# Four layers' experts as three fp32r passes a product, with split weights and four landing buffers

## The reference

```python
combine = jnp.sum(jax.nn.one_hot(idx, N_EXPERTS, dtype=jnp.float32) * gsel[..., None], axis=-2)
...
gate, up = jnp.split(jnp.einsum('ld,edf->lef', xs, w_gu), 2, axis=-1)     # 1024 -> 2 x 256
hid = jax.nn.silu(gate) * up * cw[..., None]
return jnp.einsum('lef,efd->ld', hid, w_down)                             # 256 -> 1024
```

## Time and profile before

| | us |
|---|---|
| median of 3 runs (2869.59 to 2881.02) | 2874.03 |
| the profiled execution | 2871.9 |
| its span, first to last instruction | 2870.1 |
| PE busy | 2560.3 (89%) |
| weight loads of PE busy | 1879.5 (65%) |
| DVE busy | 1432.8 (50%) |
| POOL busy | 796.8 (28%) |
| ACT busy | 753.7 (26%) |

### The profile page before, as it was taken

One profiled execution on the slowest core, in us unless ns is written; L12 is line 12 of the kernel. 1 busy time (PEld: TensorE's weight loads), 2 busy tenths in 40 slices (PEclk: granted clock), 3 DMA queues, 4 the chain that ended last, 5 costly groups with the idle time before them and its releaser, 6 DMA issues.

```text
span 2870.1 us, 30129 instructions
## 1 busy us (share of the span) xinstructions
PE 2560.3 (89%) x11915; PEld 1879.5 (65%) x11915; DVE 1432.8 (50%) x1956; ACT 753.7 (26%) x1265; POOL 796.8 (28%) x429
## 2 busy tenths in 40 slices
PE   5779889998898979999988977789999799889997
PEld 3779864445887778744458966675444699864444
DVE  6446553334746776533446489874333426740013
ACT  1133130012553451300023344422100333130111
POOL 3356400001543434000015478730000357500000
PEclk8889989998999999899989988989999899989998
DMA  7533639892331236398925311144999143438880
GB/s 267 173 118 92 212 147 348 331 369 98 107 118 35 83 93 184 148 351 330 368 81 182 118 36 36 34 176 176 345 344 349 35 129 103 147 117 297 301 297 35
DMA packets 291851, 524.41 MB, mean 183 GB/s; under 512 B 9472, under 2 KB 141056, under 8 KB 291328
## 3 DMA queue, kind: packets, MB, share of 16 engines
q1 hardware_dynamic: 288256, 519.33, 51.5%
q10 hardware_dynamic: 3456, 3.15, 0.3%
HBM read 517.73 MB, written 4.72 MB: 182 GB/s over the span
## 4 chain that ended last, share of the span: by engine, by line
PE 73%; DVE 14%; ACT 4%; DMA 3%; issue 3%; POOL 2%; SPq 0%; ACTq 0%; DVEq 0%
PE ps L1895 23%; PE ps L1912 12%; PE ps L1642 6%; PE ps L1643 6%; PE ps L1644 6%; DVE macc L1984 3%; PE ps L1707 2%; POOL wlo L1574 2%; DVE uw L1335 2%; PE ps L1665 1%; PE ps L1833 1%; PE ps L1667 1%; PE ps L1666 1%; PE ps L1857 1%; PE ps L1858 1%
## 5 line engine op out<-in xcount | busy, mean ns | idle before, releaser
L1574 POOL TENSOR_TENSOR wlo<-ring,whi 128x1024 fp32r<-128x1024 f32 x202 | 533.2, 2655 | 1467.5 <-ACT whi L1441 1467.5
L1895 PE MATMUL ps<-ring,xg 128*128 128x512 f32 x1536 | 702.7, 595 | 0.0
L1895 PEld LDWEIGHTS ps<-ring,xg 128*128 128x128 f32 x1536 | 280.5, 190 | 296.7 <-issue 296.3
L1984 DVE SCALAR_TENSOR_TENSOR macc<-ring,cond_s,macc 128x1024 f32<-128x1024 f32 x322 | 440.9, 1429 | 10.6 <-DMA ring<-w_mod 10.6
L2202 DVE SCALAR_TENSOR_TENSOR hid<-ps,cws,sg 128x256 f32<-128x256 f32 x96 | 46.4, 483 | 652.7 <-ACT sg L1535 652.7
L1912 PE MATMUL ps<-ring,hidt 128*128 128x512 f32 x768 | 353.4, 604 | 2.3 <-ACT hidt L1510 2.3
L1642 PE MATMUL ps<-hh,whi 128*128 128x384 f32 x840 | 301.3, 359 | 29.6 <-POOL wlo L1574 16.9
L1643 PE MATMUL ps<-hl,whi 128*128 128x384 f32 x840 | 289.9, 345 | 0.0
L1644 PE MATMUL ps<-hh,wlo 128*128 128x384 f32 x840 | 289.5, 345 | 0.0
L1441 ACT ACTIVATE whi<-ring 128x1024 fp32r<-128x1024 f32 x202 | 207.0, 1054 | 312.0 <-DMA ring<-gmlp_w_out 111.7
L1912 PEld LDWEIGHTS ps<-ring,hidt 128*128 128x128 f32 x768 | 147.7, 194 | 185.2 <-issue 185.2
(11 more groups left out here) (358 smaller groups left out, 4040.9 us busy)
## 6 DMA issues: line engine op xcount, KB each, us to landing
ring<-moe_w_gu SPq DMA_DIRECT2D x192, 1024.0 KB, 8.2
ring<-w_mod SPq DMA_DIRECT2D x96, 1024.0 KB, 8.2
ring<-moe_w_down SPq DMA_DIRECT2D x96, 1024.0 KB, 6.2
ring<-gmlp_w_in SPq DMA_DIRECT2D x32, 1024.0 KB, 5.8
ring<-ssd_w_in SPq DMA_DIRECT2D x21, 1024.0 KB, 5.2
ring<-hgrn_w_in SPq DMA_DIRECT2D x20, 1024.0 KB, 5.3
ring<-gmlp_w_out SPq DMA_DIRECT2D x16, 1024.0 KB, 5.8
ring<-ssd_w_out SPq DMA_DIRECT2D x8, 1024.0 KB, 6.2
```

The source lines that it names most:

```text
L1574: pool.tensor_tensor(split_sub(wlo, s0), raw_sub(s0), split_sub(whi, s0).bitcast(F32), ALU.subtract).then_inc(S["lo_ready"], 1)
L1895: ins = pe.matmul(ps[:, s % 2, :], xg[:, w, k, :], whole(what, s, 4)[:, k % 4, :], start=(k == 0), stop=(k == KD - 1))
L1984: ins = dve.scalar_tensor_tensor(out=macc[:, v, :], in0=w[:, k, :], scalar=by, in1=macc[:, v, :], op0=ALU.mult, op1=ALU.add)
```

## The change

`SPLIT` names the layers whose experts are done in the new way: all four. Their weight chunks become narrow, as in the mixers, with two subs each (a sub of A or B is two rows of 128x512, a sub of D one row of 1024), and so do the modulation chunks that ride along: four landing slots for all of them. ACT makes the highs; of the lows, POOL makes those of first subs and DVE those of second subs (`low` in the DVE block; vector_lows and pool_lows count them apart, which is why every wait for lo_ready in the mixers now goes by pool_lows). A slot of an expert chunk is free once both of its lows are made, that of a modulation chunk once its four multiply-adds are. xg and hidt get a high part (ACT, as before) and a low part by DVE (xgl, hidtl). PE does three passes for each product. DVE's four multiply-adds are parted: two before hid of their step, two after. The core of the diff (the renamed waits and the parts for layers outside SPLIT are left out):

```diff
+SPLIT = (0, 1, 2, 3)
...
+    rows_of = -1 if l not in SPLIT else 2 if what == "D" else 4
+    part(("mod", l + 1) if what == "M" else (l, what), 1, 0 if what == "M" else rows_of, l not in SPLIT)
...
+    vector_lows, pool_lows = [0], [0]
+    for s in order_of:
+        by_vector = chunk_rows[s // 2] in (2, 4) and s % 2 == 1
+        vector_lows.append(vector_lows[-1] + by_vector)
+        pool_lows.append(pool_lows[-1] + (not by_vector))
...
+    elif chunk_rows[p] in (2, 4):
+        sp.wait_ge(S["lo_ready"], pool_lows[nth[2 * p] + 2])
+        sp.wait_ge(S["low_ready"], vector_lows[nth[2 * p] + 2])
...
+    def expert_used(eng, l, what, s):
+        if l in SPLIT:
+            eng.wait_ge(S["sub_done"], nth[sb((l, what), 2 * s + 1)] + 1)
+        else:
+            eng.wait_ge(S["moe_used"], used[places[l, what][s]])
...
+    ahead = lambda what, i: feed(sb((l, what), i) + 3) if l in SPLIT and i >= 0 else None
     for s in range(STEPS):
+        ahead("A", 2 * s)
+        ahead("A", 2 * s + 1)
         if s:
             hidden_over(s - 1)
-        act.wait_ge(S["moe_used"], used[places[l, "B"][s]])
+        ahead("B", 2 * s)
+        ahead("B", 2 * s + 1)
+        expert_used(act, l, "B", s)
         if s >= 2:
             act.wait_ge(S["hid_ready"], n0 + s - 1)
         act.activation(sg[:, s % 2, :], ps[:, s % 2, 0:DE], ACT.Silu).then_inc(S["sg_ready"], 1)
+        ahead("D", 2 * s - 2)
+        ahead("D", 2 * s - 1)
...
+    if vector_lows[n + 1] > vector_lows[n]:
+        return
...
+    claim(at_bank, "xgl_ready", 16 * SPLIT.index(l) + 2 * k + part + 1)
...
+    def wide_product(out, xhi, xlo, s0, half, first, last):
+        cut = slice(512 * half, 512 * half + 512)
+        hi, lo = whi[:, nth[s0] % SPL, cut], wlo[:, nth[s0] % SPL, cut]
+        pe.matmul(out, xhi, hi, start=first, stop=False)
+        pe.matmul(out, xhi, lo, start=False, stop=False)
+        return pe.matmul(out, xlo, hi, start=False, stop=last)
...
+    s0 = sb((l, what), 2 * s + k // 2 % 2)
+    if k % 2 == 0:
+        low_in(s0)
+    ins = wide_product(ps[:, s % 2, :], xgh[:, w, k, :], xgl[:, w, k, :], s0, k % 2, k == 0, k == KD - 1)
+    if k % 2:
+        ins.then_inc(S["sub_done"], 1)
+    if s and k == 1:
+        hidden_over(s - 1)
...
+    for k in range(2):
+        s0 = sb((l, "D"), 2 * s + k)
+        low_in(s0)
+        for h in range(2):
+            ins = wide_product(ps[:, OUT_BANKS[w % 2][h], :], hidth[:, s % 2, k, :], hidtl[:, s % 2, k, :], s0, h,
+                               e == 0 and k == 0, e == EG - 1 and k == 1)
+        ins.then_inc(S["sub_done"], 1)
+    return
...
+    def low(l, what, i):
+        n = nth[sb((l, what), i)]
+        s0 = order_of[n]
+        dve.wait_ge(S["hi_ready"], n + 1)
+        dve.tensor_tensor(split_sub(wlo, s0), raw_sub(s0), split_sub(whi, s0).bitcast(F32), ALU.subtract).then_inc(S["low_ready"], 1)
...
+    def rows_low(k):
+        if l in SPLIT:
+            dve.wait_ge(S["xg_ready"], 16 * l + 2 * k + 2)
+            for part, (a, b) in enumerate(((0, NG), (NG, NW))):
+                dve.tensor_tensor(xgl[:, a:b, k, :], ps[:, 2 * ((k + 1) % 2) + part, 0:(b - a) * P].rearrange("p (w n) -> p w n", n=P),
+                                  xgh[:, a:b, k, :].bitcast(F32), ALU.subtract).then_inc(S["xgl_ready"], 1)
...
+    def hidden_rest(s):
+        dve.wait_ge(S["hidt_ready"], n0 + s + 1)
+        dve.tensor_tensor(hidtl[:, s % 2, :, :].rearrange("p a n -> p (a n)"), ps[:, 2, (s % 2) * DE:(s % 2 + 1) * DE],
+                          hidth[:, s % 2, :, :].rearrange("p a n -> p (a n)").bitcast(F32), ALU.subtract).then_inc(S["hidtl_ready"], 1)
...
+    if l in SPLIT and s:
+        low(l, "B", 2 * s + 1)
+        hidden_rest(s - 1)
+        if e == 1 and w:
+            window_low(w - 1)
+        low(l, "D", 2 * s - 1)
+    if l in SPLIT and s in mods:
+        mod_chunk(MODC * (l + 1) + MOD_GROUP + mods[s], range(0, 2))
...
+    if l in SPLIT and s + 1 < STEPS:
+        low(l, "A", 2 * s + 3)
     if last_of(s - 2):
         mod_take(6 * (l + 1) + 1 + mods[s - 2] // MOD_GROUP)
     if s in mods:
-        mod_chunk(MODC * (l + 1) + MOD_GROUP + mods[s])
+        mod_chunk(MODC * (l + 1) + MOD_GROUP + mods[s], range(2, 4) if l in SPLIT else range(4))
```

More of the change, by code:

```diff
@@ L266, in trunk @@
         olo = ar("olo", [P, NW, D], F32R, 24)
+        xgh = ar("xgh", [P, NW, KD, P], F32R, 48)
+        xgl = at("xgl", [P, NW, KD, P], F32R, hoff)
         spread = ar("spread", [P, NT, NW * P], F32R, 24)
@@ L279, in trunk @@
         hidt = yr("hidt", [P, 2, 2, P], F32, 4)
+        hidth = yr("hidth", [P, 2, 2, P], F32R, 4)
+        hidtl = yr("hidtl", [P, 2, 2, P], F32R, 9)
         srow = yr("srow", [P, T], F32, 6)
@@ L1409, in split_waits @@
             for l in range(DEPTH - 1):
-                if n == nth[end_of_experts(l)]:
+                if l not in SPLIT and n == nth[end_of_experts(l)]:
                     eng.wait_ge(S["moe_used"], used[places[l, "D"][-1]])
@@ L1904, in down @@
                     w, e = divmod(s, EG)
[L1905 to L1906 removed]
+                    if l not in SPLIT:
+                        chunk_in(pe, places[l, "D"][s])
+                    pe.wait_ge(S[turned], t0 + s + 1)
                     if e == 0:
@@ L1965, in _, with mod_chunk @@
             link = chain.link
-            def mod_chunk(m):
+            def mod_chunk(m, parts=range(4)):
                 q, steps = m % MOD_GROUP, 4 * (MOD_GROUP * group_of_mac(m // MOD_GROUP) + m % MOD_GROUP)
                 c = mod_at[steps // 4]
-                chunk_in(dve, c)
                 w = ring[:, slot_of[c], :].rearrange("p (k n) -> p k n", k=2)
-                if m == 0:
-                    dve.wait_ge(S["cond_ready"], 1)
-                elif q == 0:
-                    dve.wait_ge(S["mod_summed"], m // MOD_GROUP)
-                for k in range(2):
-                    for v in range(2):
-                        by = cond[:, 2 * q + k, v:v + 1]
-                        if q == 0 and k == 0:
-                            ins = dve.tensor_scalar(macc[:, v, :], w[:, k, :], by, None, ALU.mult)
-                        else:
-                            dve.wait_ge(S["mac_step"], steps + 2 * k + v - 1)
-                            ins = dve.scalar_tensor_tensor(out=macc[:, v, :], in0=w[:, k, :], scalar=by, in1=macc[:, v, :],
-                                                           op0=ALU.mult, op1=ALU.add)
-                        ins.then_inc(S["mac_step"], 1)
@@ new lines, in mod_chunk @@
+                if 0 in parts:
+                    chunk_in(dve, c)
+                    if m == 0:
+                        dve.wait_ge(S["cond_ready"], 1)
+                    elif q == 0:
+                        dve.wait_ge(S["mod_summed"], m // MOD_GROUP)
+                for k, v in (divmod(i, 2) for i in parts):
+                    by = cond[:, 2 * q + k, v:v + 1]
+                    if q == 0 and k == 0:
+                        ins = dve.tensor_scalar(macc[:, v, :], w[:, k, :], by, None, ALU.mult)
+                    else:
+                        dve.wait_ge(S["mac_step"], steps + 2 * k + v - 1)
+                        ins = dve.scalar_tensor_tensor(out=macc[:, v, :], in0=w[:, k, :], scalar=by, in1=macc[:, v, :],
+                                                       op0=ALU.mult, op1=ALU.add)
+                    ins.then_inc(S["mac_step"], 1)
@@ L2107, in route @@
                 pairs = rt[:, 2:4, :, :].rearrange("p a t e -> p (a t e)")[:, 0:72].rearrange("p (g e) -> p g e", e=6)
+                if l in SPLIT:
+                    low(l, "A", 1)
+                    low(l, "B", 1)
                 dve.wait_ge(S["route_ready"], l + 1)
```

90 lines of the change are left out of this document (56 added, 34 removed).

## The result

| | before | after |
|---|---|---|
| median | 2872.01 us (2869.59 to 2881.02, 4 runs) | 3381.45 us (3373.25 to 3387.71, 4 runs) |
| span of the profiled execution | 2870.1 us | 3377.1 us |
| PE busy, DVE busy | 2560.3, 1432.8 us | 2571.8, 2226.2 us |
| ACT busy, POOL busy | 753.7, 796.8 us | 1324.6, 1583.4 us |

The ratio of the times is 1.1755 (95% interval 1.1732 to 1.1777): 17.6% slower, as forecast.

A forecast was written before the change was run, and what follows sets the result against it. TensorE (PE) was taken to bound the kernel now; after the change, loads and POOL/DVE turns would. 2871.9 us + 488 (layers 0 to 2) + 19 (layer 3) + 4 (sorted rows) = 3383, stated as 3380 us, range 3110 to 3500.

The forecast's parts named there:

- The load path: Layers 0 to 2: moe_w_down loads wait for multiply-adds queued behind the previous moe_w_down's low on DVE; three-step period 51.9 us, chance 0.55.
- D0: The moe_w_down chunk of step 0 in the hand-built three-step period; its load, sent second, lands at 9.0 us.
- D1: The next step's moe_w_down chunk in that period; its load waits for the second pair of multiply-adds, lands at 27.7 us.
- the first rival: Expert stages, layers 0 to 2: both delays overlap wholly, 3157 us; load path alone closes at about 43 us; chance 0.20.
- The turns: Expert stages: POOL's lows, DVE's lows and multiply-adds run one after another, sharing SBUF ports; floor 42.9 us per three steps.
- the list: Hand-made path through one three-step period of layers 0 to 2, assuming DVE keeps the turn while it has work; 51.9 us.
- A2: POOL's low of step 2's A chunk, placed after the first step's multiply-adds and hid, 16.3 to 18.7 us.
- A4: POOL's low of step 4's A chunk, placed after the later multiply-add pair and hid, ending at 48.2 us.
- the rival "worse": Expert stages: POOL gets a turn after each DVE instruction, about 2 x 2.3 us more a period, 3490 us; chance 0.13.
- The term of layers 0 to 2: Expert stages with modulation chunks: 24 periods of 51.9 us in place of 31.56, +488 us.
- Layer 3: Expert stage without modulation chunks: floor 10.9 us a step, taken as 11.3, +19 us (ends -46 and +84).
- Sorted rows: DVE's added xgl instructions beside the gather: +1 us a layer, +4 us in all (ends 0 and +37).

## Why the prediction was right, step by step

**The sum.** The mechanism was the forecast one; that the sum came so close is in part luck. Its three terms were +488, +19 and +4 us; measured, hid to hid and by what is left over, they are +503, -8 and +12. The errors of -15, +27 and -8 us leave 4 us, 511 for the span's 507.

**The load path.** It was the likeliest case, and it is what the chip did. Mark by mark in the period from 644.63 us, in us from there, predicted and measured: D0 landed 9.0 and 8.1; the pair of multiply-adds behind its low over at 16.3 and 19.3; the second pair 22.4 and 23.3; D1 landed 27.7 and 28.2; the third down chunk sent for 32.6 and 32.8; two multiply-adds over 45.8 and 50.4; end 51.9 and 54.3. The runs without the loads (-282 us) and with another order of DVE's queue (-248 us) show the one half of it, the run without POOL's turns (-275 us) the other, and each leaves 42 to 45 us, where the first rival had about 43.

**The turns.** One assumption of the list was wrong: "DVE keeping the turn while it has work". POOL, once its input is there, takes a turn between two multiply-adds, so the pairs take 6.7 us and not 2.5. Most of that came back, since the POOL turns that I had put after the pairs (A2, A4) are then over, and D0 landed a microsecond sooner. That leaves +2.4 us a period. It is the rival "worse" in part: where that had +4.6 us a period, half of it came. The Trainium skill (SBUF — State Buffer, two separate sides) says that whichever of the two starts first has the shared ports for its whole instruction and the other blocks. The trace agrees but for a small part: in the 6.75 us from 657.19 end a POOL low that has 2.31 us left, another of 2.39 and two multiply-adds, of 1.27 each where they run alone. One after the other these are 7.24 us, so some 0.5 us of them overlap.

**The term of layers 0 to 2.** +488 predicted, +503 measured from hid to hid. The two figures don't count alike: from hid to hid there are 23 steps, and my sum has 24. The 31.56 us of three steps before left out what PE does for mod_sum after each fourth modulation chunk: the stages before are 249.0 us for 23 steps, 10.83 each and not 10.52. (Layer 3's, which have no mod_sum, are 10.37.) For 23 steps at 51.9 us a period the path gives 397.9 - 249.0 = 148.9 us a layer, +447 in all; with 54.3 it is +502, which is what was measured. So like for like the term was 55 us too small: the step after was 0.8 us longer than in my sum. The step before was 0.3 us longer too, and the sum had one step a layer more; these two make up for 41 of the 55 us, and that is luck.

**Layer 3: mis-sized.** +19 predicted, -8 measured, inside its ends. The floor was 3 x (2.41 + 1.22) = 10.9 us a step; the steps took 10.0. The timeline after, layer 3:

```profile
3187.07 43.54 POOL L1603 TENSOR_TENSOR wlo<-ring,whi 128x1024 fp32r<-128x1024 f32 x13
...
3191.87 6.38 DVE L2062 TENSOR_TENSOR wlo<-ring,whi 128x1024 fp32r<-128x1024 f32 x2
```

Thirteen lows of POOL stand in 43.54 us without a gap: 3.35 us each with the DVE low in between, not 3.63. Two instructions that were read alone (2.41 and 1.22) cost 0.28 us less when they hand over to each other. In the chain above as well a DVE low right behind another instruction counts 1.13 (695.39). The 0.4 us of slack that I had added wasn't needed either: in these 43.54 us POOL always has a low to make.

**Sorted rows and the rest.** +4 predicted, +12 left over. Of it 8.3 us stand before layer 0's first hid and 4.9 before layer 1's. The kernel with SPLIT = (3,), which has nothing new there, is also 3.0 us later at layer 0's first hid, so that much is no effect of the rows; the rest was not taken apart.

**What the profile was to show.** The clock (0.83), the DMA rate (208 for about 210 GB/s), the mean of the multiply-adds (1907 ns for over 1.6 us), layer 3's stage within 20 us, and stages far over 350 us came as said. POOL has 1583 us for about 1500: 288 lows of experts at 2.73 us rather than 2.41. PE's 2571.8 us for 2310 is a miss of 262. A small part is my subtraction: the 1056 us of L1895 and L1912 count twice where both lines have a record; counted once they are 1028 us. The large part is that the passes got longer: counted once as well, the expert products take 1018 us in the kernel after, where I had 806. Some 22 us of the miss stay open. In the four stages PE was busy for 986 us before and for 993 after, so the three passes gave PE next to nothing back here. From 622 us on in the chain after, the three passes of a product stand 0.43 us apart, not the 0.233 of the earlier trace rows:

```profile
622.08 0.43 PE ps L1916
622.51 0.43 PE ps L1917
```

PE had been busy for 3.2 of the 9.3 us up to 621.3 (it waited for wlo), at a granted clock of 0.96; from 621.3 to 627.2 the clock is 0.50, and 0.99 from there on. 0.43 us for 512 columns is the lower level, 1.2 GHz, 0.23 the higher. In this stretch PE is on the chain with 15 us, for a reason that my path lacked: the first multiply-add of the next group waits until PE has summed macc (L1736, among the passes), so after a fourth modulation chunk the path can go through PE. I had put the lower clock at "a few us a layer". PE isn't on the chain at all from 644.63 to 698.95, but in layer 0's whole stage 183 passes of the experts are, with 60 us, and 95 of them take over 0.3 us: by an estimate from these durations and 0.233 us a pass, 19 us more than at the higher clock.

**A link that I had missed.** hidth of step s - 1 stands behind the high of D's first sub in ACT's in-order queue, and hidtl behind hidth. So they too wait until moe_w_down lands (hidtl 367.9 us, 72 times; hidth at 653.66 in the timeline above, right behind the high at 652.70). On this path it cost little, since DVE's low of the same chunk was to wait anyway.

## What to carry to other kernels

Fewer passes on the bounding engine are a gain only up to the next bound, so price the helpers first, and price DVE and POOL together where both read and write SBUF: 576 subtractions on DVE alone were 154 us faster than the same shared half and half. When landing slots are halved, write down for every load which instruction frees its slot and what stands ahead of that instruction on its engine; a load whose freeing stands behind another load's arrival makes a round trip, and moving four instructions was worth 248 us here. Where two delays meet in one chain, removing one shows only a part of its worth (282 and 275 us apart, 658 together), so try both before giving the idea up, and the idea itself where it has no such rider (layer 3 alone, all lows by DVE: 1.1% faster).

## What the runs showed of the hardware that I had not expected

- POOL gets a turn between two instructions of DVE that are both ready: pairs of multiply-adds of 6.7 us around two POOL lows, at 657.19 and 688.27. In the stages of layers 0 to 2 a POOL low begins 35 times while a multiply-add runs that has another right behind it, and all 35 times it goes before that one. The earlier trace rows had one stretch each way: of the four multiply-adds at 74.16 the last two went before a POOL low that began at 76.42. What decides between the two is not shown.
- A DVE low and a POOL low in turn cost 3.35 us together (43.54 us for 13), 0.28 less than the two read alone.
- A DVE instruction with one wide SBUF input and a column is held up as well: back, a 128x384 comparison, takes 0.41 us or, beside POOL's lows, 2.56 (11 of its 24 executions are that long; with all lows by DVE none is). Those that read ps are not: hidtl, one input in ps, has a mean of 421 ns, and 0.42 us where it begins inside a POOL low, at 674.18. The row that I had read this from (L2082 at 235.88 in the earlier trace rows) couldn't show it, as its instruction began before POOL's. The timeline after:

```profile
673.95 2.34 POOL L1603 TENSOR_TENSOR wlo<-ring,whi 128x1024 fp32r<-128x1024 f32 x1 [11.10 <-ACT whi L1461]
674.18 0.42 DVE L2293 TENSOR_TENSOR hidtl<-ps,hidth 128x256 fp32r<-128x256 f32 x1 [5.19 <-ACT hidth L1530]
...
680.58 2.39 POOL L1603 TENSOR_TENSOR wlo<-ring,whi 128x1024 fp32r<-128x1024 f32 x1 [0.96 <-ACT whi L1461]
680.62 2.56 DVE L2324 TENSOR_SCALAR back<-srow,pcol 128x384 fp32r<-128x384 f32 x1
...
698.84 0.41 DVE L2324 TENSOR_SCALAR back<-srow,pcol 128x384 fp32r<-128x384 f32 x1
```
